# Two-layer hybrid decoder step on one core: fifth product kept in its own tile, and three reorderings in the in-product stage

## The chip, the cores and the metric

The kernel runs on one core of a Trainium2 chip. The metric is the device time of one execution in microseconds (us), as the median of several runs. One execution was also profiled; its rows are what the argument is made from.

## What is computed

Two layers. Layer 0 mixes tokens with two convolution mixers, layer 1 with dilated sliding-window attention; each layer ends in a ConvFFN, and a last RMSNorm follows. The change touches only the ConvFFN:

```python
def conv_ffn(h, st, w_in, wc, w_down):
    z = h @ w_in                                   # 1024 -> 2 * 2816
    g, st_new = causal_dwconv(z[..., :D_FF], st, wc)   # width 3, per channel
    return (jax.nn.silu(g) * z[..., D_FF:]) @ w_down, st_new
```

There are 1056 token columns (1024 of the prompt, 8 samples of 4 tokens), kept as three thirds of 352 columns. `h` is the normalised input of the layer; the kernel multiplies by the RMS factor (`rst`) after the product.

## The kernel before

**The in-product stage.** The 2816 channels of `z` are made in 22 rounds (`NJ`), j = 0 to 21, in each layer. One round makes 128 gate and 128 up channels for all tokens. It uses a recursive scheme with eleven block products in place of twelve. Each product is 12 TensorE matmuls of 352 columns (4 pieces of the contraction times 3 pieces of split precision), so a round has 132. In TensorE's order they are: P1, G3A, U3A, P5, P2, G3B, P6, P3, P7, U3B, P4 (the `STEP_...` constants; `step_full` counts them). P1, P6, P7 and P4 add up in one PSUM tile `za`, P5 and P3 in `ZB`, P2 in `ZC`, G3A and G3B in `ZG`, U3A and U3B in `zu`. `za` and `zu` alternate between two places from round to round.

**Operands.** Eight weight blocks are made ready for each round, one round ahead: A11, A21, A12, A22 straight from `w_raw`, and four sums S1, S2, S4, S3 that VectorE makes (`quad_sum`, S2 with two instructions). For each block ScalarE rounds the high part (`quad_hi`, L1283) and GpSimd takes the low part (`quad_lo`, L1710). P6 uses S2, P3 uses S4, P7 uses S3, U3B and P4 use A22.

**Intermediate results.** ScalarE copies three partial sums out of PSUM (`copy_part`, L1296): number 0 is `za` after P1, number 1 is `ZB` after P5, number 2 is `za` after P6. P6 waits for copy 0, P3 for copy 1, P7 for copy 2. VectorE then combines (`combine`): number 0 (L2069) after P2, 1 (L2076) after G3B, 2 (L2079) after P3, 3 (L2082, tile `u2`) after P7; P4 waits for combine 3. Combine 0 also has to precede copy 2, which overwrites `part`.

**Behind the products.** `scale_gate` (L2090) multiplies the gate by the factor, `taps` (L2101 to L2111) applies the width-3 convolution, ScalarE applies SiLU (`silu`, L1485), GpSimd multiplies by the factor (`silu_scale`, L1730), and VectorE multiplies by the up branch (`hidden`, L2131, three instructions, the last of which reads `u2`). `hidden(j-1)` falls in round j. The result `tmp` is stored by a DMA on SP's queue (`store_hid`), and reloaded for the down projection (`load_hid`, L609). The last round has a few instructions of the down projection mixed in: `hidden_lo(0, 0)` stands on VectorE ahead of combine 3 and needs the reload.

Every engine executes its instructions in the order in which they are written out by hand; semaphores join the engines. In the trace the tile `u2` appears as `u`, and `ZB` and `za` as `reg`; `ob` is the second place of `zu`. The line that the argument turns on is in `copy_part`, for copy 1:

```python
if which == 1:
    act.wait_ge(prod_ok, 3 * jj)      # all three instructions of hidden(j-1)
    dst, src = u2[:, :], ZB
```

Of the kernel before, what the change touches and what calls it, by code (L numbers as in the profile page):

```python
# [22 lines left out]
F32 = mybir.dt.float32  # L23
# [175 lines left out]
def build(nc, xT, wstream, par, ident_d, ones_d, stA, stB, stF, kva, kvb, wtab, sbias, cache_k, cache_v,  # L199
# [3 lines left out]
    with ExitStack() as ctx:  # L203
        def place(name, shape, dt, off):
            size = int(np.prod(shape[1:])) * 4
            return nc.alloc_sbuf_tensor_at(name, shape, dt, offset=off), off + (size + 31) // 32 * 32
# [34 lines left out]
        spare, off = place("spare", [P, T], F32, off)  # L241
        mean_s, off = place("mean_s", [P, NS], F32, off)
        cs, off = place("cs", [P, 16], F32, off)
        prod, off = place("prod", [P, NB, NQ // 2, KA], F32, off)
        AS, off = place("AS", [P, CA, NB, PAD + NQ], F32, off)
        tmp, off = place("tmp", [P, T], F32, off)
# [1 line left out]
        acc, off = place("acc", [P, T], F32, off)  # L248
        assert off <= nc.sbuf_usable_end
        gbuf = g3  # L250
        rst2, o2 = place("rst2", [P, T], F32, SX0)
        assert o2 <= SX0 + 4 * NJ * NB * (KF - 1 + NQ)
        sf_st, o2 = place("sf_st", [P, NJ, NB, KF - 1], F32, SPARE0)
# [986 lines left out]
        def _(act):  # L1240
# [44 lines left out]
            def copy_part(L, j, which):  # L1285


                jj = NJ * L + j
                act.wait_ge(step_full, step_at(L, j, (STEP_P1, STEP_P5, STEP_P6)[which]))
                if which == 1:  # L1290
                    act.wait_ge(prod_ok, 3 * jj)
                    dst, src = u2[:, :], ZB
                else:
                    act.wait_ge(comb_ok, 4 * jj + 1 if which else max(4 * jj - 1, 0))
                    dst, src = part[:, :], ZA[j % 2]
                nc.scalar.activation(dst, src, ACT.Copy).then_inc(part_ok, 1)  # L1296
# [181 lines left out]
            def ffn(L):  # L1478
                first_tiles(L)

                def silu(j):
                    jj = NJ * L + j
                    act.wait_ge(conv_ok, jj + 1)
                    act.wait_ge(prod_ok, 3 * jj)
                    nc.scalar.activation(sil[:, PAD:], acc[:, :], ACT.Silu).then_inc(silu_ok, 1)  # L1485

                def down_hi(d):


                    u = U_FFN[L] + 2 * NJ + d  # L1490
                    act.wait_ge(step_full, step_at(L, NJ - 1, (STEP_G3B, STEP_P3, STEP_P4)[d]))
                    split_hi(act, u)

                def hidden_hi(g):
                    act.wait_ge(hid_in[g % 2], 32 * ((6, 5)[g % 2] * L + g // 2 + 1))
                    for c in range(2):
                        nc.scalar.activation(hid[:, g % 2, c, 0, :], hraw[:, g % 2, c, 1, :], ACT.Copy).then_inc(hid_hi, 1)

                def last_copy():


                    act.wait_ge(step_full, step_at(L, NJ - 1, STEP_P4))
                    for x, z in enumerate((ZA, ZU)):
                        nc.scalar.activation(up_last[:, x, :], z[(NJ - 1) % 2], ACT.Copy).then_inc(last_up, 1)

                for j in range(NJ):
                    more = j < NJ - 1
                    if j > 0:
                        copy_part(L, j, 0)
                        quad_hi(L, j, Q_S3)  # L1510
                        quad_hi(L, j, Q_A22)
                        copy_part(L, j, 1)
                        if more:
                            quad_hi(L, j + 1, Q_A11)
                        else:
                            down_hi(0)
                        copy_part(L, j, 2)
                        if more:
                            quad_hi(L, j + 1, Q_A21)
                    if more:  # L1520
                        for q in (Q_S1, Q_A12, Q_S2, Q_S4):
                            quad_hi(L, j + 1, q)
                    else:
                        hidden_hi(0)
                        down_hi(1)
                        last_copy()
                        down_hi(2)
                    silu(j)
                hidden_hi(1)
                for g in range(NG - 1):  # L1530
                    for x in range(2):
                        hi_after(act, down_unit(L, g, x))
                    if g + 2 < NG:
                        hidden_hi(g + 2)
                s2 = 2 if L == 0 else 4
                for m in range(KD):
                    if L == 1 and m == KD - 1:
                        act.wait_ge(sum_ok, SQ0[4] + m - 1)
                        for t in range(NT):
                            act.wait_ge(h_third, t + 1)  # L1540
                            nc.scalar.activation(sqb[(SQ0[4] + m) % 2][:, t * TS:(t + 1) * TS],
                                                 h[:, m, t * TS:(t + 1) * TS], ACT.Square).then_inc(sq_third, 1)
                        return
                    h_ready(act, s2, m)
                    square(s2, m, h[:, m, :])
                    if L == 0:
                        gain_hi(2, 2, m)
                    if m % 4 == 3:
                        hi_after(act, down_unit(L, NG - 1, m // 4))
# [128 lines left out]
        def _(pool):  # L1678
# [34 lines left out]
            def ffn(L):  # L1713
# [14 lines left out]
                def silu_scale(j):  # L1728
                    pool.wait_ge(silu_ok, NJ * L + j + 1)
                    nc.gpsimd.tensor_tensor(sil[:, PAD:], sil[:, PAD:], rst[:, :], ALU.mult).then_inc(silr_ok, 1)  # L1730

                s = (1, 3)[L]
                for m in range(KD):
                    if m % 2 == 0 or L == 1:
                        lo_after(pool, U_OUT + 4 + m // 2 if L == 0 else U_WO + m)
                    add_square(s, m)
                for j in range(NJ):
                    if j > 0:
                        quad_lo(L, j, Q_S3)
                        quad_lo(L, j, Q_A22)  # L1740
                        silu_scale(j - 1)
                    if j < NJ - 1:
                        for q in (Q_A11, Q_A21, Q_S1, Q_A12):
                            quad_lo(L, j + 1, q)
                        if j > 0:
                            history(j)
                        for q in (Q_S2, Q_S4):
                            quad_lo(L, j + 1, q)
                        if j == 0:
                            history(j)  # L1750
                    else:
                        split_lo(pool, down_unit(L, 0, 0))
                        history(j)
                        silu_scale(j)
                        split_lo(pool, down_unit(L, 0, 1))
                        split_lo(pool, down_unit(L, 1, 0))
# [34 lines left out]
        def _(dve):  # L1791
# [219 lines left out]
            def ffn(L):  # L2011
# [48 lines left out]
                def combine(j, which):  # L2060


                    jj = J0 + j
                    dve.wait_ge(step_full, step_at(L, j, (STEP_P2, STEP_G3B, STEP_P3, STEP_P7)[which]))
                    if which == 0:
                        dve.wait_ge(part_ok, 3 * jj + 1)
                        dve.wait_ge(conv_ok, jj)
                        dve.wait_ge(hist_ok, 3 * jj)
                        ins = nc.vector.tensor_tensor(third(gbuf[:, PAD:], 0), ZC, part[:, :], ALU.add)  # L2069
                    elif which == 1:  # L2070
                        dve.wait_ge(hist_ok, 3 * jj)
                        g = third(gbuf[:, PAD:], 2)
                        if j == 0:
                            ins = nc.vector.tensor_copy(g, ZG)
                        else:
                            ins = nc.vector.tensor_tensor(g, ZG, third(rst, 2), ALU.mult)  # L2076
                    elif which == 2:
                        dve.wait_ge(part_ok, 3 * jj + 3)
                        ins = nc.vector.tensor_tensor(third(gbuf[:, PAD:], 1), ZB, part[:, :], ALU.add)  # L2079
                    else:  # L2080
                        dve.wait_ge(part_ok, 3 * jj + 2)
                        ins = nc.vector.tensor_tensor(u2[:, :], ZA[j % 2], u2[:, :], ALU.add)  # L2082
                    ins.then_inc(comb_ok, 1)

                def scale_gate(j):
# [113 lines left out]
                for j in range(NJ):  # L2199
# [11 lines left out]
                    if not more:  # L2211
                        hidden_lo(0, 0)
                    combine(j, 3)
                    if more:
                        quad_sum(j + 1, Q_S2)
                    else:
                        hidden_lo(0, 1)
                    if j == 0:
                        factor_parts((5, 9)[L])
                        quad_sum(1, Q_S4)  # L2220
                        scale_gate(0)
                    taps(j)
                    if more and j > 0:
                        quad_sum(j + 1, Q_S4)
                for g in range(NG - 1):
                    for x in range(2):
# [327 lines left out]
```

## Time and profile before

| what | value |
|---|---|
| median of 3 runs | 2655.68 us (2654.19 to 2655.82) |
| the profiled execution | 2654.6 us, span of the trace 2652.8 us |
| TensorE matmul busy | 2547.8 us, 96% of the span |
| VectorE, ScalarE, GpSimd busy | 1651.5 (62%), 798.5 (30%), 946.4 us (36%) |
| mean granted TensorE clock | 0.988 |
| chain that ended last | TensorE 64%, VectorE 16%, GpSimd 11%, issue 6% |

The span is the time between the first and the last instruction in the trace; the execution's own time is 1.8 us longer. The granted clock is a share of TensorE's full clock (1.0 is 2.4 GHz, 0.5 is 1.2 GHz). The in-product stage lies at about 376 to 881 us in layer 0, and 1868 to 2373 us in layer 1.

### The profile page before, as it was taken

What the parts mean: (1) busy time and instruction counts of PE and PEld (TensorE: products, weight loads), DVE (VectorE), ACT (ScalarE), POOL (GpSimd) and SP (SyncE); (2) the same over time, 40 slices, a digit from 0 to 9 for tenths busy, and PEclk for the clock granted to TensorE, in tenths of its full rate; (3) what the DMA queues carried; (4) which work ended last, traced back from release to release, by engine and by line L of the source; (5) the groups of instructions that cost most, each with busy time, mean ns of one, the idle gap of its engine ahead of it and who ended that gap; (6) DMA issues with size and microseconds to landing.
All of it is one profiled execution on the core that took longest, in us unless ns stands there. A gap on an engine that the chain in (4) does not pass through costs nothing.

```text
span 2652.8 us, 41667 instructions
## 1 busy us (share of the span) xinstructions
PE 2547.8 (96%) x17036; PEld 2379.0 (90%) x17036; DVE 1651.5 (62%) x2593; ACT 798.5 (30%) x1400; POOL 946.4 (36%) x635
## 2 busy tenths in 40 slices
PE   8999988999999999999999999989799999999997
PEld 8999987999999999987777777769799999999997
DVE  6999777666655655565565555564756556655555
ACT  5111343333333211233333333343433333331112
POOL 1000125666666322241000101123366666652222
PEclk9999998999999999999999999999999999999998
DMA  4111102444443544435344444432187888874321
GB/s 150 42 39 48 43 9 65 139 138 140 136 137 135 192 163 153 160 137 174 121 158 152 131 172 143 167 121 100 32 262 264 268 278 262 273 272 167 97 74 74
DMA packets 106557, 383.93 MB, mean 145 GB/s; under 512 B 23936, under 2 KB 41216, under 8 KB 103936
## 3 DMA queue, kind: packets, MB, share of 16 engines
q1 hardware_dynamic: 106368, 381.26, 43.3%
q8 instruction: 136, 2.23, 0.3%
q14 instruction: 53, 0.43, 0.1%
HBM read 339.15 MB, written 176.04 MB: 194 GB/s over the span
## 4 chain that ended last, share of the span: by engine, by line
PE 64%; DVE 16%; POOL 11%; issue 6%; ACT 2%; DMA 1%; DVEq 0%; SPq 0%; ACTq 0%; POOLq 0%
PE reg L824 19%; PE reg L771 11%; PE reg L1080 9%; PE reg L968 8%; POOL wq L1710 8%; DVE acc L2103 4%; POOL sil L1730 3%; PE reg L897 3%; PE reg L1060 3%; PE ob L1116 3%; DVE wqr L2044 2%; DVE tmp L2131 2%; PE reg L1033 1%; PE reg L1101 1%; PE ob L1101 1%
## 5 line engine op out<-in xcount | busy, mean ns | idle before, releaser
L968 PE MATMUL reg<-xo,wq 128*128 128x352 f32 x5280 | 877.0, 326 | 52.0 <-ACT u L1296 21.8
L968 PEld LDWEIGHTS reg<-xo,wq 128*128 128x128 f32 x5280 | 855.6, 190 | 67.1 <-ACT u L1296 33.7
L824 PE MATMUL reg<-hid,w_sp 128*128 128x352 f32 x3150 | 510.3, 324 | 0.5 <-DVE h L1830 0.5
L824 PEld LDWEIGHTS reg<-hid,w_sp 128*128 128x128 f32 x3150 | 509.9, 189 | 0.8 <-issue 0.8
L485 POOL TENSOR_TENSOR w_sp<-w_raw,w_sp 128x1024 fp32r<-128x1024 f32 x63 | 174.4, 2770 | 745.9 <-ACT w_sp L480 725.5
L1830 DVE TENSOR_TENSOR h<-reg,h 128x1056 f32<-128x1056 f32 x199 | 250.1, 1257 | 275.3 <-PE reg L824 225.6
L1710 POOL TENSOR_TENSOR wq<-wqr,wq 128x512 fp32r<-128x512 f32 x168 | 254.2, 1533 | 183.5 <-DVE wqr L2048 177.5
L771 PE MATMUL reg<-xs,w_sp 128*128 128x352 f32 x1872 | 308.6, 326 | 10.4 <-DVE xs L1819 9.7
L771 PEld LDWEIGHTS reg<-xs,w_sp 128*128 128x128 f32 x1872 | 304.3, 189 | 13.6 <-issue 13.1
L1710 POOL TENSOR_TENSOR wq<-w_raw,wq 128x512 fp32r<-128x512 f32 x168 | 242.1, 1450 | 148.6 <-ACT wq L1283 148.6
L1080 PE MATMUL reg<-xs,w_sp 128*128 128x352 f32 x1512 | 279.5, 332 | 0.4 <-DVE VT L2257 0.4
L1080 PEld LDWEIGHTS reg<-xs,w_sp 128*128 128x128 f32 x1512 | 240.5, 188 | 18.1 <-issue 18.0
L1283 ACT ACTIVATE wq<-wqr 128x512 fp32r<-128x512 f32 x176 | 110.7, 629 | 376.1 <-DVE wqr L2045 185.5
L480 ACT ACTIVATE w_sp<-w_raw 128x1024 fp32r<-128x1024 f32 x83 | 87.8, 1058 | 449.0 <-PE reg L824 291.0
L503 POOL TENSOR_TENSOR w_sp<-w_raw,w_sp 128x1024 fp32r<-128x1024 f32 x21 | 50.0, 2379 | 475.8 <-ACT w_sp L498 456.6
L2131 DVE TENSOR_TENSOR tmp<-reg,sil 128x352 f32<-128x352 f32 x64 | 31.5, 521 | 287.8 <-POOL sil L1730 287.8
L1583 ACT ACTIVATE pT<-ob 128x512 f32<-128x512 f32 (+1 forms) x96 | 47.1, 491 | 329.0 <-PE ob L1101 329.0
L2103 DVE SCALAR_TENSOR_TENSOR acc<-g,pt,acc 128x1024 f32<-128x1024 f32 x88 | 115.1, 1308 | 3.1
L1283 ACT ACTIVATE wq<-w_raw 128x512 fp32r<-128x512 f32 x176 | 109.8, 626 | 17.3 <-PE reg L968 17.2
L2298 DVE COPY pT<-reg 128x512 f32<-128x512 f32 (+1 forms) x96 | 53.4, 557 | 97.8 <-PE reg L1101 97.3
L2275 DVE CUSTOM_DVE_ANT_0 neg_s<-reg,wt 128x512 f32<-128x512 f32 (+1 forms) x192 | 107.3, 559 | 6.9 <-DVE eps L2263 0.3
L1576 ACT ACTIVATE neg_s<-neg_s,nmx 128x896 f32<-128x896 f32 (+7 forms) x128 | 98.1, 768 | 35.9 <-DVE nmx L2280 33.2
(248 smaller groups left out, 2972.8 us busy)
## 6 DMA issues: line engine op xcount, KB each, us to landing
w_raw<-in_wstream SPq DMA_DIRECT2D x192, 512.0 KB, 3.6
out_sv<-in_cache_v SPq DMA_DIRECT2D x16, 4088.0 KB, 16.0
out_sk<-in_cache_k SPq DMA_DIRECT2D x16, 4088.0 KB, 16.2
kvr<-in_kva SPq DMA_DIRECT2D x16, 2048.0 KB, 9.0
kvr<-in_kvb SPq DMA_DIRECT2D x16, 1536.0 KB, 7.0
hid_spill<-tmp SPq DMA_DIRECT2D x44, 528.0 KB, 3.0
hraw<-hid_spill SPq DMA_DIRECT2D x44, 528.0 KB, 4.5
wt<-in_wtab SPq DMA_DIRECT2D x16, 512.0 KB, 5.3
```

The source lines that it names most:

```text
L480: nc.scalar.activation(w_sp[:, u % 3, 0, :], w_raw[:, u % 3, :], ACT.Copy).then_inc(w_hi, 1)
L485: nc.gpsimd.tensor_tensor(w_sp[:, u % 3, 1, :], w_raw[:, u % 3, :], w_sp[:, u % 3, 0, :].bitcast(F32), ALU.subtract).then_inc(w_lo, 1)
L771: mm = nc.tensor.matmul(out[:, t, :], w[:, wh, k * P:(k + 1) * P], xs[:, xh, k, t * TS:(t + 1) * TS], start=(n == 0 and wh + xh == 0), sto ...
L824: mm = nc.tensor.matmul(out[:, t, :], w[:, wh, kk * 512 + m * P:kk * 512 + (m + 1) * P], hid[:, par_g, kk, xh, t * TS:(t + 1) * TS], start ...
L968: mm = nc.tensor.matmul(out, w[:, wh, k * P:(k + 1) * P], xo[:, o, xh, k, :], start=(first and k == 0 and wh + xh == 0), stop=(k == 3 and ...
L1080: mm = nc.tensor.matmul(dense[:, t, :], w[:, wh, k * P:(k + 1) * P], xs[:, xh, k, t * TS:(t + 1) * TS], start=(k == 0 and wh + xh == 0), s ...
L1283: nc.scalar.activation(wq[:, ring(L, j, q), 0, :], quad_src(L, j, q), ACT.Copy).then_inc(wq_hi, 1)
L1576: nc.scalar.activation(neg_s[:, hh, 0:w], neg_s[:, hh, 0:w], ACT.Exp, bias=nmx[:, m, hh:hh + 1], scale=-1.0, accum_out=lsum[:, 0, hh:hh + ...
L1710: nc.gpsimd.tensor_tensor(wq[:, r, 1, :], quad_src(L, j, q), wq[:, r, 0, :].bitcast(F32), ALU.subtract).then_inc(wq_lo, 1)
L1830: nc.vector.tensor_tensor(tok(h[:, m, :]), region(r), tok(h[:, m, :]), ALU.add).then_inc(free, 1)
L2103: chain(nc.vector.scalar_tensor_tensor(out=y, in0=g, scalar=w[k], in1=y, op0=ALU.mult, op1=ALU.add))
L2275: nc.vector.tensor_tensor_reduce(out=neg_s[:, hh, lo:lo + w], in0=S[hh][:, 0:w], in1=wt[:, hh, t0:t0 + w], scale=-1.0, scalar=3.0e38, op0= ...
```

## The change

1. **Fifth product.** Copy 1 (P5) goes to a tile of its own, `p5`, laid over the storage of `prod`, which only layer 0's long convolution uses. It no longer waits for `hidden(j-1)`, but for the previous round's combine 3, which reads `p5`. Combine 3 now adds `p5` to `za` and writes `u2`.
2. **SiLU on ScalarE.** In rounds 2 to 21 `silu(j-1)` follows copy 0 of round j; before, it stood ahead of it. `silu(0)` follows copy 1 of round 1.
3. **Factor on GpSimd.** In rounds 2 to 21 `silu_scale(j-1)` stands ahead of the low parts of S3 and A22 instead of behind them. In round 1 nothing is moved.
4. **Taps on VectorE.** `taps(j)` stands ahead of both instructions of `quad_sum(j+1, S2)` rather than behind them. In round 0 `quad_sum(1, S4)` moves ahead of `factor_parts` (the two reciprocals).

```diff
+        p5, o2 = place("p5", [P, TS], F32, PROD0)
...
                 if which == 1:
-                    act.wait_ge(prod_ok, 3 * jj)
-                    dst, src = u2[:, :], ZB
+                    act.wait_ge(comb_ok, 4 * jj)
+                    dst, src = p5[:, :], ZB
...
                     if j > 0:
                         copy_part(L, j, 0)
+                        if j > 1:
+                            silu(j - 1)
                         quad_hi(L, j, Q_S3)
                         quad_hi(L, j, Q_A22)
                         copy_part(L, j, 1)
+                        if j == 1:
+                            silu(0)
...
-                    silu(j)
+                        silu(j)
...
                 for j in range(NJ):
+                    if j > 1:
+                        silu_scale(j - 1)
                     if j > 0:
                         quad_lo(L, j, Q_S3)
                         quad_lo(L, j, Q_A22)
-                        silu_scale(j - 1)
+                    if j == 1:
+                        silu_scale(0)
...
                         dve.wait_ge(part_ok, 3 * jj + 2)
-                        ins = nc.vector.tensor_tensor(u2[:, :], ZA[j % 2], u2[:, :], ALU.add)
+                        dve.wait_ge(prod_ok, 3 * jj)
+                        ins = nc.vector.tensor_tensor(u2[:, :], ZA[j % 2], p5[:, :], ALU.add)
...
                     combine(j, 3)
-                    if more:
-                        quad_sum(j + 1, Q_S2)
-                    else:
+                    if not more:
                         hidden_lo(0, 1)
                     if j == 0:
+                        quad_sum(1, Q_S2)
+                        quad_sum(1, Q_S4)
                         factor_parts((5, 9)[L])
-                        quad_sum(1, Q_S4)
                         scale_gate(0)
                     taps(j)
                     if more and j > 0:
+                        quad_sum(j + 1, Q_S2)
                         quad_sum(j + 1, Q_S4)
```

ScalarE, the turn from round 1 to round 2 of layer 0, before: L1485 is `silu(1)`, the first `part` copy 0 of round 2, `u_75` copy 1; the two instructions between them are the high parts of S3 and A22.

```order
L1283 ACTIVATE wq<-wqr 128x512 x2
L1485 ACTIVATE sil<-acc 128x1056
L1296 ACTIVATE part<-reg 128x352
L1283 ACTIVATE wq<-wqr 128x512
L1283 ACTIVATE wq<-w_raw 128x512
L1296 ACTIVATE u_75<-reg 128x352
```

The same place after the change (L1299 is the copy, L1488 SiLU, L1286 the high part, `p_73` the new tile):

```order
L1286 ACTIVATE wq<-wqr 128x512 x2
L1299 ACTIVATE part<-reg 128x352
L1488 ACTIVATE sil<-acc 128x1056
L1286 ACTIVATE wq<-wqr 128x512
L1286 ACTIVATE wq<-w_raw 128x512
L1299 ACTIVATE p_73<-reg 128x352
```

SiLU has changed places with copy 0; the copy of the fifth product stands where it stood. In round 1 of a layer, after the change, ScalarE has this (copy 0, the two high parts, copy 1, a load of the activation table, `silu(0)`, the high part of round 2's A11, copy 2):

```order
L1299 ACTIVATE part<-reg 128x352
L1286 ACTIVATE wq<-wqr 128x512
L1286 ACTIVATE wq<-w_raw 128x512
L1299 ACTIVATE p_73<-reg 128x352
L1488 ACT_TABLE_LOAD
L1488 ACTIVATE sil<-acc 128x1056
L1286 ACTIVATE wq<-w_raw 128x512
L1299 ACTIVATE part<-reg 128x352
```

Before, the table load and `silu(0)` stood ahead of all of these. GpSimd, a later turn of rounds, before: the low parts of S2, S4 and S3, that of A22, then the factor (L1730).

```order
L1710 TENSOR_TENSOR wq<-wqr,wq 128x512 x3
L1710 TENSOR_TENSOR wq<-w_raw,wq 128x512
L1730 TENSOR_TENSOR sil<-sil,rst 128x1056
L1710 TENSOR_TENSOR wq<-w_raw,wq 128x512 x2
```

After the change (L1717 the low part, L1737 the factor):

```order
L1717 TENSOR_TENSOR wq<-wqr,wq 128x512 x2
L1737 TENSOR_TENSOR sil<-sil,rst 128x1056
L1717 TENSOR_TENSOR wq<-wqr,wq 128x512
L1717 TENSOR_TENSOR wq<-w_raw,wq 128x512 x3
```

The factor now has two low parts fewer ahead of it in this turn, and S3 and A22 have it ahead of them.

## Rows read from the trace of the kernel before

**Rows 1.** Windows, all rounds between the stage's start and end, both layers

```profile
core 0: us, PE busy (x) PEld busy (x) DVE busy (x) ACT busy (x) POOL busy (x), PEclk, DMA share, GB/s
440.00:860.00 420.00, 412.75 (x2556) 407.58 (x2555) 254.94 (x370) 128.08 (x231) 287.47 (x229) 1.00 0.43 134
1932.00:2352.00 420.00, 412.82 (x2559) 407.65 (x2558) 254.39 (x370) 128.81 (x232) 288.68 (x231) 1.00 0.81 267
```

**Rows 2.** Chain that ended last: start us, us, what (TensorE without a wait)

```profile
440.11 27.07 PE reg L968 x168
```

**Rows 3.** Timeline of one round, layer 0: start us, us, engine, instruction, [idle before]

```profile
553.56 0.69 DVE L2048 TENSOR_TENSOR wqr<-w_raw,wqr 128x512 f32<-128x512 f32 x1
...
554.40 4.12 POOL L1710 TENSOR_TENSOR wq<-wqr,wq 128x512 fp32r<-128x512 f32 x3 [4.08 <-DVE wqr L2048]
...
558.48 1.29 POOL L1710 TENSOR_TENSOR wq<-w_raw,wq 128x512 fp32r<-128x512 f32 x1
559.74 2.05 POOL L1730 TENSOR_TENSOR sil<-sil,rst 128x1056 f32<-128x1056 f32 x1
561.82 0.96 DVE L2131 TENSOR_TENSOR tmp<-reg,sil 128x352 f32<-128x352 f32 x2 [6.96 <-POOL sil L1730]
...
563.30 0.46 ACT L1296 ACTIVATE u<-reg 128x352 f32<-128x352 f32 x1 [6.02 <-DVE tmp L2131]
...
563.82 4.14 PE L968 MATMUL reg<-xo,wq 128*128 128x352 f32 x24 [0.36 <-ACT u L1296]
...
568.00 0.52 DVE L2082 TENSOR_TENSOR u<-reg,u 128x352 f32<-128x352 f32 x1 [0.18 <-PE reg L968]
568.45 1.07 DVE L2044 TENSOR_TENSOR wqr<-w_raw 128x512 f32<-128x512 f32 x1
...
569.55 1.67 DVE L2045 TENSOR_TENSOR wqr<-wqr,w_raw 128x512 f32<-128x512 f32 x1
...
571.14 0.74 DVE L2101 TENSOR_SCALAR acc<-g,pt 128x1024 f32<-128x1024 f32 x1
...
571.92 2.61 DVE L2103 SCALAR_TENSOR_TENSOR acc<-g,pt,acc 128x1024 f32<-128x1024 f32 x2
```

**Rows 4.** Timeline, rounds 0 and 1 of layer 0

```profile
407.87 6.54 DVE L1812 RECIPROCAL rst<-rst 128x1024 f32<-128x1024 f32 x1
...
416.21 1.28 ACT L1485 ACT_TABLE_LOAD   x1
...
418.42 3.59 DVE L2103 SCALAR_TENSOR_TENSOR acc<-g,pt,acc 128x1024 f32<-128x1024 f32 x2
...
424.79 3.89 PE L968 MATMUL reg<-xo,wq 128*128 128x352 f32 x12 [6.35 <-ACT part L1296]
...
431.89 6.29 PE L968 MATMUL reg<-xo,wq 128*128 128x352 f32 x24 [3.22 <-ACT u L1296]
...
438.02 2.09 PE L968 MATMUL ob<-xo,wq 128*128 128x352 f32 x12
```

**Rows 5.** Timeline, the same place in layer 1

```profile
1917.26 3.89 PE L968 MATMUL reg<-xo,wq 128*128 128x352 f32 x12 [5.34 <-ACT part L1296]
...
1929.86 2.07 PE L968 MATMUL ob<-xo,wq 128*128 128x352 f32 x12
```

**Rows 6.** Windows, rounds 1 (from P6 on), both layers; columns as in rows 1

```profile
424.79:431.89 7.10, 3.88 (x12) 3.43 (x12) 1.99 (x5) 1.49 (x4) 4.53 (x3) 0.50 0.48 148
...
1917.26:1924.37 7.11, 3.89 (x12) 3.44 (x12) 2.00 (x5) 1.50 (x4) 4.53 (x3) 0.70 0.48 150
```

**Rows 7.** Timeline, the last round of layer 0

```profile
868.43 1.20 SPq L609 DMA_DIRECT2D hraw<-hid_spill  x2
...
868.59 4.14 PE L968 MATMUL reg<-xo,wq 128*128 128x352 f32 x24 [0.49 <-ACT u L1296]
...
874.60 2.06 ACT L1497 ACTIVATE hid<-hraw 128x1056 fp32r<-128x1056 f32 x2 [4.76 <-DMA hraw<-hid_spill]
...
877.46 3.51 PE L968 MATMUL reg<-xo,wq 128*128 128x352 f32 x12 [2.81 <-DVE u L2082]
```

**Rows 8.** Timeline, the last round of layer 1

```profile
2369.21 3.89 PE L968 MATMUL reg<-xo,wq 128*128 128x352 f32 x12 [3.33 <-DVE u L2082]
```

More of the change, by code:

```diff
@@ L243, in build @@
         cs, off = place("cs", [P, 16], F32, off)
+        PROD0 = off
         prod, off = place("prod", [P, NB, NQ // 2, KA], F32, off)
@@ L250, in build @@
         gbuf = g3
+        p5, o2 = place("p5", [P, TS], F32, PROD0)
+        assert o2 <= PROD0 + 4 * NB * (NQ // 2) * KA
         rst2, o2 = place("rst2", [P, T], F32, SX0)
```

## The prediction

> **What bounds the stage now.** I read the windows first, to see how much TensorE has left to gain. Between the stage's ragged start and end, 420 us hold 2556 matmuls [rows 1], 21.69 us for a round of 132. Where nothing holds TensorE, 168 matmuls take 27.07 us [rows 2], 161.1 ns each, so a round at its pace is 21.27 us. The granted clock is 1.00 throughout. The missing 0.4 to 0.5 us a round is a wait, and it is all that the change can win in a steady round.
>
> Then one round's timeline, for what closes the loop [rows 3]. The last sum S4 is made at 553.56. GpSimd takes four low parts (S2, S4, S3, A22) from 554.40 to 559.77, and the factor until 561.80. Only then can `hidden` run, whose third instruction frees `u2` at 563.2; ScalarE copies the fifth product at 563.30, and P3, the first half of the 24 matmuls at 563.82, starts 0.36 us late. P7 ends at 567.98, combine 3 runs, and S2, taps and S4 follow on VectorE until the next low parts start one round later. So a loop VectorE, GpSimd, VectorE, ScalarE, TensorE sets the period, a little above TensorE's own. VectorE and GpSimd are busy for 255 and 287 of 420 us [rows 1]: it is their order that binds.
>
> Last, the ragged ends. In round 1 TensorE idles 6.35 us before P6, because ScalarE holds copy 0 behind `silu(0)`, then 3.22 us before P3 [rows 4]; the layer-1 idle before P6 is 5.34 us [rows 5]. The clock falls with it: 0.50 in 424.79:431.89 [rows 6], P6's 12 matmuls take 3.89 us instead of 1.93. In the last round P4 waits 2.81 us (3.33 in layer 1) and then takes 3.51 (3.89) us [rows 7, 8].
>
> **Steady rounds.** I count time t from P7's end. In the new loop combine 3 ends at t+0.47; taps follow. Their stretch cost 0.74 + 2.61 + about 0.8 us for the samples [rows 3]. In their new place three low parts and the state copies of GpSimd run beside them, where S2's instructions now take 1.07 and 1.67 us against 0.69 for the like S4 [rows 3]. The nearest row for taps beside GpSimd is the pair in round 0, 3.59 us against 2.61 [rows 4, 3]. I add 1.3 us to taps and take 1.3 off S2, which moves out of that place: S4 ends at t+8.0, as before (553.56+0.69 against P7's end one period before). GpSimd: S2 and S4 low (half of the 5.37 us that the four take) until t+10.8, the factor until t+12.8. SiLU is ready: after S4's high part (0.6) and copy 0 (0.45), 1.07 us, t+10.3. `hidden` and combine 0: 1.4 + 0.43, until t+14.7. Nothing on TensorE waits for `hidden` now but through combine 0, copy 2 and P7. Copy 2 needs P6, which ends at t+17.4 (nine products after P7: U3B, P4, then seven of the next round), and P7 starts at t+19.3. Even with the 0.5 of the copy there are 4.1 us between the chain and P7. Copy 1 (P5 ends at t+11.6) has until P3, t+17.4; S3's and A22's low parts, now behind the factor, end at t+15.5, needed at 19.3 and 21.3. The weight reload behind A22's low part leaves 1.9 us later; its block is wanted in the round after next, and hides. So steady rounds are TensorE's, 21.27 us. From P4 of round 1 (438.02 + 1.93 = 439.95) to P3 of round 21 (868.59) [rows 4, 7] lie 428.64 us and 12 + 19·132 + 84 = 2604 matmuls, 419.6 us at the pace: **9.0 us** a layer, 18.0 in both.
>
> **Start of the stage.** S4 of round 1 no longer stands behind the reciprocals (6.54 us [rows 4]), and copy 0 not behind `silu(0)`, so P6 starts without a wait at 418.44 and ends at 420.4. P3 needs copy 1, behind the high parts of S3 and A22, and S3's sum stands on VectorE behind taps(0): reciprocals until 415.5, `scale_gate` until 416.8, taps (beside less of GpSimd than now, 4.5 us) until 421.3, S3 422.0, two high parts and the copy until 423.6. P3 starts 8.2 us sooner than now. But P7 is behind a longer chain: table load 1.28 us, SiLU 1.07, the factor 2.05, `hidden` 1.4, combine 0, copy 2: 430.45. The idle time of 3.2 us before P3 becomes 4.9 before P7. No row has exactly this idle; 5.34 and 6.35 us were each followed by 12 matmuls at the lower clock (3.89 us) [rows 4, 5], so I take P7 at 3.87. P4 of round 1 then starts at 430.45 + 3.87 + 1.93 = 436.3 in place of 439.95: **3.7 us**. In layer 1 the chain is the same 1492.4 us later: 1928.7 against 1929.86 + 1.93 = 1931.8: **3.1 us**. Bounds: P7 at full clock, 1.9 more a layer; U3B slow as well, 1.9 less.
>
> The table load is now on this path; its row is 1.28 us [rows 4], which the sum uses. The Trainium skill (ScalarE: Activation LUTs, What ACT_TABLE_LOAD costs) adds a drain of about 1.38 us to the 1.28 of the load. By that page, as an estimate, the start would gain 1.4 us less a layer and the kernel take 2.8 us longer than forecast.
>
> **End of the stage.** The chain is `hidden(20)`, store, reload (868.43 to 874.60 [rows 7]), high and low part, combine 3, P4. `hidden(20)` ends two low parts sooner, some 2.7 us, and the reload is behind it in SP's queue and behind nothing else. Combine 3 comes at about 874.2 in place of 876.9, U3B ends near 873.9: P4 waits 0.4 us, in layer 1, by the same count, 0.95. With so short a wait I take P4 at full clock, 1.93 us. Gains: 2.4 + 1.6 = **4.0** and 2.4 + 1.9 = **4.3 us**. If the clock falls all the same, 3.5 less in all. In the down projection behind it VectorE's chain (taps, SiLU, factor, `hidden(21)`) moves up with combine 3; I take nothing for it, at most 1 us lost.
>
> **Sum.** 18.0 + 3.7 + 3.1 + 4.0 + 4.3 = 33.1 us off the profiled execution's 2654.6: 2621.5. The median of the runs lies 1.1 above that execution: **2622.5 us**. The rest (`p5` for `u2` as target and source) changes no duration: the same sizes and memories.
>
> **Rivals.** (a) *The loop closes again, shorter.* Taps or low parts run slower side by side than I have them, and half of the steady gain stays lost: 2631.5. It needs 4.1 us more in the chain than counted before it bites, and 4.3 to halve the gain; the rows show 1.0 us for the pair. 0.08. (b) *The change doesn't do what it says in steady rounds*: the 0.4 us is TensorE's own gap at this place, or another wait (S4's low part) ends there too. Then only the ends gain, 15.1 us: 2640.5. Against it, P3's idle ends with the copy, and the other operands have been ready for over 4 us. 0.05. (c) *Slower.* Taps are put beside GpSimd's low parts, and each of the three long ones waits for a whole GpSimd instruction of up to 1.9 us, S2 as much as now: 5.7 − 1.3 + 1.3 + 1.7 for GpSimd's own low parts is 7.4 us, 3.3 over the slack of 4.1, a period of 24.6 us, 2.8 more than now in 39 rounds: +109, less 15 at the ends, 2750. It decides from 4.6 us on. The pair in round 0 lost only 1.0 us beside the same work [rows 4]. 0.04. The Trainium skill (SBUF — State Buffer, SBUF: two separate sides) has it that a VectorE instruction with two SBUF inputs and a GpSimd one exclude each other for the whole instruction; by that rule (c) is what would happen, and the trace agrees in the sign (1.67 against 0.69 us for one of S2), not in the size here. (d) Losses and gains cancel within 0.2%, which is what a measurement of this kernel can tell: needs 28 us of the 33 lost, 0.02. My forecast has 0.81.
>
> **Range.** Downwards: P7 at full clock in both layers (3.9) and no wait at the end (1.4) give 2617; with half a per mille of the measurement, 2615. Upwards: U3B slow too (3.9), P4's clock lost (3.5), 1 us in the down projection, and (a) half: 2634. Faster than by 0.2%: 0.94; within it 0.02; slower 0.04.
>
> **What would show it.** Steady windows: 2556 matmuls in 412 us, no wait of TensorE on a ScalarE copy. `hidden`'s wait for the factor falls from 6.96 to some 4 us. Round 1: one idle of about 3 us before P3, one of about 5 before P7, released by copy 2, and a stretch at clock 0.5 behind it. P4 of round 21 with a wait under 1 us and 1.93 us long. I am wrong if a steady round keeps a wait before P7 or P3, if taps take much over 5.5 us, or if the clock falls elsewhere.

## The result, and the profile after

The changed kernel takes 2626.94 us (median of 4 runs, 2623.84 to 2632.76), the kernel before 2655.68: a ratio of 0.9896, interval 0.9875 to 0.9916, 28.7 us less. The forecast was 2622.5, range 2615 to 2634. The profiled execution is the slowest of the four, 2632.76 us (span 2631.0), 21.8 less than the profiled one of before.

The windows of the steady rounds, changed kernel, columns as in [rows 1]:

```profile
440.00:850.00 410.00, 410.00 (x2547) 410.00 (x2546) 256.28 (x369) 130.25 (x232) 294.67 (x229) 1.00 0.45 137
1932.00:2342.00 410.00, 410.00 (x2547) 410.00 (x2546) 252.76 (x364) 129.31 (x229) 294.37 (x230) 1.00 0.78 270
```

TensorE is busy in all of the 410 us, where it had been in 412.8 of 420. The chain that ended last shows the same; it now stays on TensorE from one product to the next:

```profile
438.84 27.07 PE reg L971 x168
...
481.37 27.07 PE reg L971 x168
```

Two rounds are 42.53 us, 21.27 each, as the pace of [rows 2] gives. One round's timeline, against [rows 3]:

```profile
564.94 0.51 DVE L2093 TENSOR_TENSOR u<-reg,p 128x352 f32<-128x352 f32 x1
565.37 1.35 DVE L2112 TENSOR_SCALAR acc<-g,pt 128x1024 f32<-128x1024 f32 x1
...
566.76 2.60 DVE L2114 SCALAR_TENSOR_TENSOR acc<-g,pt,acc 128x1024 f32<-128x1024 f32 x2
...
571.67 0.69 DVE L2058 TENSOR_TENSOR wqr<-w_raw,wqr 128x512 f32<-128x512 f32 x1
...
572.51 2.86 POOL L1717 TENSOR_TENSOR wq<-wqr,wq 128x512 fp32r<-128x512 f32 x2 [4.42 <-DVE wqr L2058]
...
575.34 2.05 POOL L1737 TENSOR_TENSOR sil<-sil,rst 128x1056 f32<-128x1056 f32 x1
...
576.14 0.47 ACT L1299 ACTIVATE p<-reg 128x352 f32<-128x352 f32 x1 [0.74 <-PE reg L971]
...
577.42 0.53 DVE L2142 TENSOR_TENSOR tmp<-reg,sil 128x352 f32<-128x352 f32 x1 [4.45 <-POOL sil L1737]
...
578.94 0.51 DVE L2079 TENSOR_TENSOR g<-reg,part 128x352 f32<-128x352 f32 x1
...
581.94 0.47 ACT L1299 ACTIVATE part<-reg 128x352 f32<-128x352 f32 x1 [4.82 <-PE reg L971]
```

Read it from combine 3 at 564.94, which starts 0.4 us after P7's end. S4 ends at 572.4, 7.4 us on; two low parts and the factor end at 577.4; combine 0 ends at 579.45, 14.95 us after P7's end (14.7 counted). The copy of the fifth product, at 576.14, and copy 2, at 581.94, each wait for a product of TensorE, no longer for VectorE.

The start of the stage in layer 0, against [rows 4], and the same places in layer 1, against [rows 5]:

```profile
408.91 1.57 DVE L2058 TENSOR_TENSOR wqr<-w_raw,wqr 128x512 f32<-128x512 f32 x1
...
413.39 7.79 PE L971 MATMUL reg<-xo,wq 128*128 128x352 f32 x48
425.06 1.28 ACT L1488 ACT_TABLE_LOAD   x1
425.09 3.89 PE L971 MATMUL reg<-xo,wq 128*128 128x352 f32 x12 [3.91 <-ACT p L1299]
426.35 1.08 ACT L1488 ACTIVATE sil<-acc 128x1056 f32<-128x1056 f32 x1
...
432.22 3.89 PE L971 MATMUL reg<-xo,wq 128*128 128x352 f32 x12 [3.24 <-ACT part L1299]
435.91 2.93 PE L971 MATMUL ob<-xo,wq 128*128 128x352 f32 x12
...
1907.25 2.20 PE L971 MATMUL reg<-xo,wq 128*128 128x352 f32 x12 [2.86 <-ACT p L1299]
...
1914.38 3.89 PE L971 MATMUL reg<-xo,wq 128*128 128x352 f32 x12 [4.93 <-ACT part L1299]
```

P5 to P6 run through (the 48 matmuls), then P3 and P7 wait, and P7 is slow in both layers, P3 in one. The windows over P3, P7 and U3B of layer 0 and over P3 and P7 of layer 1 show which clock they had (the third figure from the end):

```profile
424.70:429.00 4.30, 3.89 (x12) 3.43 (x12) 0.00 (x0) 3.23 (x4) 3.54 (x3) 0.50 0.57 168
...
432.00:436.00 4.00, 3.78 (x13) 3.78 (x14) 2.76 (x4) 1.82 (x4) 3.24 (x3) 0.50 0.33 135
436.00:438.80 2.80, 2.80 (x14) 2.80 (x13) 2.62 (x3) 0.00 (x0) 2.80 (x4) 0.69 0.00 0
...
1907.20:1909.40 2.20, 2.15 (x12) 1.91 (x12) 0.00 (x0) 2.18 (x2) 1.72 (x2) 1.00 0.51 209
1914.30:1918.20 3.90, 3.82 (x13) 3.82 (x14) 2.62 (x3) 1.69 (x4) 3.28 (x3) 0.50 1.10 392
```

The end of the stage in layer 0, against [rows 7]: P4's wait, then the down projection with a wait of its own.

```profile
865.23 2.17 PE L971 MATMUL reg<-xo,wq 128*128 128x352 f32 x12 [1.07 <-DVE u L2093]
...
867.24 11.76 PE L827 MATMUL reg<-hid,w_sp 128*128 128x352 f32 x72
...
873.72 5.06 POOL L488 TENSOR_TENSOR w_sp<-w_raw,w_sp 128x1024 fp32r<-128x1024 f32 x2
874.40 4.76 DVE L2142 TENSOR_TENSOR tmp<-xraw,sil 128x352 f32<-128x352 f32 x2
...
880.91 19.37 PE L827 MATMUL reg<-hid,w_sp 128*128 128x352 f32 x109 [1.91 <-DVE h L1840]
```

### The profile page after: what moved, and what is told of

Same layout as the page of the kernel before. It is cut to its first block, busy times and chain, and to the rows that moved or that the text cites. A ratio compares the mean times of both kernels' runs of the same rounds, so it can differ in the third digit from the quotient of the medians.

```text
span 2631.0 us, 41669 instructions
## 1 busy us (share of the span) xinstructions
PE 2545.5 (97%) x17036; PEld 2387.4 (91%) x17036; DVE 1657.9 (63%) x2593; ACT 802.9 (31%) x1400; POOL 956.5 (36%) x635
## 4 chain that ended last, share of the span: by engine, by line
PE 88%; DVE 7%; issue 2%; ACT 1%; DMA 1%; POOL 1%; DVEq 0%; SPq 0%; ACTq 0%; POOLq 0%
PE reg L971 29%; PE reg L827 19%; PE reg L774 11%; PE reg L1083 9%; PE ob L971 3%; PE reg L900 3%; PE reg L1063 3%; PE ob L1119 3%; PE reg L1036 1%; PE reg L1104 1%; PE ob L1104 1%; PE reg L1172 1%; PE reg L1159 1%; DVE neg_s L2286 1%; PE reg L794 1%
## 5 line engine op out<-in xcount | busy, mean ns | idle before, releaser
L1717 POOL TENSOR_TENSOR wq<-wqr,wq 128x512 fp32r<-128x512 f32 x168 | 232.3, 1393 | 180.0 <-DVE wqr L2058 173.1
L1717 POOL TENSOR_TENSOR wq<-w_raw,wq 128x512 fp32r<-128x512 f32 x168 | 253.1, 1516 | 111.2 <-ACT wq L1286 111.1
L1286 ACT ACTIVATE wq<-wqr 128x512 fp32r<-128x512 f32 x176 | 110.5, 628 | 383.5 <-DVE wqr L2055 338.9
L2142 DVE TENSOR_TENSOR tmp<-reg,sil 128x352 f32<-128x352 f32 x64 | 31.5, 521 | 188.1 <-POOL sil L1737 188.1
L1286 ACT ACTIVATE wq<-w_raw 128x512 fp32r<-128x512 f32 x176 | 109.4, 624 | 17.7 <-PE reg L971 17.3
```

The lines of the kernel that those rows point to most:

```text
L1286: nc.scalar.activation(wq[:, ring(L, j, q), 0, :], quad_src(L, j, q), ACT.Copy).then_inc(wq_hi, 1)
L1717: nc.gpsimd.tensor_tensor(wq[:, r, 1, :], quad_src(L, j, q), wq[:, r, 0, :].bitcast(F32), ALU.subtract).then_inc(wq_lo, 1)
```

## The experiments

Twelve kernels, each but `b4_slack` in five rounds beside the kernel before. "Undone" is meant from the changed kernel.

| label | what | median us | ratio to before, 95% |
|---|---|---|---|
| a1_full_again | the changed kernel | 2627.1 | 0.9895 (0.9880 to 0.9910) |
| a2_tile_only | only the own tile | 2628.0 | 0.9901 (0.9888 to 0.9915) |
| a3_factor_only | only the factor's place | 2630.3 | 0.9906 (0.9892 to 0.9919) |
| a4_taps_only | only VectorE's order | 2660.1 | 1.0020 (1.0011 to 1.0029) |
| b1_no_tile | own tile undone | 2625.4 | 0.9888 (0.9874 to 0.9901) |
| b2_taps_back | taps undone | 2625.9 | 0.9893 (0.9873 to 0.9912) |
| c1_s4_back | S4 of round 1 undone | 2626.5 | 0.9888 (0.9875 to 0.9902) |
| c2_silu_back | SiLU undone in rounds 2 to 21 | 2624.0 | 0.9885 (0.9871 to 0.9898) |
| b3_start_and_end | rounds 1 and 21 reordered | 2616.7 | 0.9854 (0.9841 to 0.9868) |
| c3_start | round 1 reordered | 2617.3 | 0.9856 (0.9838 to 0.9874) |
| c4_start_end_split | both, and hidden(21) spread | 2608.9 | 0.9826 (0.9807 to 0.9844) |
| b4_slack | three factor instructions more | 2862.0 | 1.0779 (1.0759 to 1.0799) |

**a1_full_again.** No edit.

> The changed kernel once more, for the spread of its runs and a second profile. Theory A (what remains of the gain varies with when TensorE's clock falls and rises around the short idle times at the stage's ends): steady rounds again 21.27 us with no wait, the medians near 2627 us, single runs between 2622 and 2633, and the second profile differs from the first in stretches at the lower clock, not in a wait. Rival B (a transfer or a wait that is late in some runs): the second profile shows one wait of several us that the first doesn't have, or the other way round.

The four runs go from 2623.7 to 2629.1, and no wait of the stage or of the down projection differs by more than 1.6 us from the first profile's (layer 1's wait in the down projection, 1.9 us instead of 0.3). One wait is new, 0.7 us before P4 of round 11 in layer 0, behind a weight block that came late. But neither theory names the larger difference, TensorE's own pace in the steady rounds. The first profile has 168 matmuls in 27.07 us throughout; the second, in layer 0:

```profile
440.36 26.69 PE reg L971 x168
```

That is 158.9 ns a matmul against 161.1, at a granted clock of 1.00 in both. The layer's 2604 matmuls take 414.7 us instead of 419.5, with the wait of 0.7 in them: 4.8 of the 6.3 us between the two profiles. Other profiles have 26.88, and b1's changes within a layer with no wait between. The first stage of the kernel, 504 matmuls in 81.53 us, is the same in every profile. What sets the pace stays open. It can hide or feign a gain of a few us in a median of four runs, so each run below is read by its trace as well, in stretches from one product to another.

**One part alone.** a2 has the lines of the change that make and use `p5` and nothing more, a3 only the factor's place:

```diff
                 for j in range(NJ):
+                    if j > 1:
+                        silu_scale(j - 1)
                     if j > 0:
                         quad_lo(L, j, Q_S3)
                         quad_lo(L, j, Q_A22)
-                        silu_scale(j - 1)
+                    if j == 1:
+                        silu_scale(0)
```

and a4 only VectorE's order (the last part of the change).

> Only the fifth product's own tile; SiLU, factor, taps and sums stand as before the change. Theory A (the chain counted from P7's end reaches copy 2 at 17.9 us, 1.4 us ahead of P7 even with four low parts in it): steady rounds at TensorE's pace, all of the 18 us; start 1 to 3 us a layer, since P3 no longer waits for the u2 tile but P6 still for SiLU; P4 of the last round waits still over 3 us. About 2633 us (2630 to 2638). Rival B (the order of the factor is what matters, the tile alone only shifts the wait to copy 2): steady rounds stay above 21.5 us, over 2642 us.

> Only the factor moved ahead of the low parts of S3 and A22 on GpSimd (rounds 2 to 21); no own tile, SiLU, taps and sums as before the change. Theory A (the chain to copy 1 gets 2.6 us shorter, ends at 14.8 us from P7's end, P3 needs it at 17.4): steady rounds at TensorE's pace, all of the 18 us; start as before the change; end as in the whole change. About 2631 us (2627 to 2637). Rival B (only the tile breaks the loop): a copy of the fifth product still ends a wait of P3, less than 6 us gained.

> Only VectorE's order changed (taps ahead of S2, and S4 of round 1 ahead of the reciprocals). Theory A (the loop holds taps, S2 and S4 in whatever order, and SiLU stands behind S4's high part): steady rounds as before, 21.7 us; the start 1 us a layer faster; about 2653 us (2650 to 2657). Rival B (earlier taps free SiLU and with it the factor): at least 8 us faster, 2647 or less.

Theory A held in the first two: TensorE has no wait from 440 to 850 us in either. The tile alone brings 26.7 us and the factor's place alone 24.4, against 27.6 for the whole change beside the same runs of before; the intervals overlap. a2 came out 5 us better than its point and 2 below its range. Part is the faster pace in layer 1 (26.88 us), part the start: from P4 of round 0 to P4 of round 1 it takes 31.6 and 30.5 us in the two layers, the whole change 33.0 and 31.5, the kernel before 35.1 and 33.4. In a2 nearly all the idle time falls ahead of P6 (6.2 us in layer 0). P7 waits 1.4 us and runs at a granted clock of 1.00:

```profile
432.14 2.18 PE L971 MATMUL reg<-xo,wq 128*128 128x352 f32 x12 [1.41 <-ACT part L1299]
```

So at the start the whole change loses to the tile alone, 1.4 and 1.0 us in the two layers (1.2 and 0.4 by a1's profile): it starts P7 1.2 us sooner, but as a slow product. It wins at the end, where a2's P4 still waits 3.2 and 2.9 us.

In a4 both theories were too kind: it is slower. All waits of its TensorE for ScalarE from 404 to 895 us, and the kernel before's:

```profile
PE reg L971 <- ACT u L1299: 15.6, 19, 3.2
PE reg L971 <- ACT part L1299: 3.9, 1, 3.9
```

```profile
PE reg L968 <- ACT u L1296: 10.9, 19, 3.2
PE reg L968 <- ACT part L1296: 6.4, 1, 6.4
```

The start gains 2.4 us in layer 0, by the shorter wait before P6; in layer 1 that wait stays (5.2 against 5.3 us) and the start loses 1.0. The waits for the copy of `u2` grow by 0.25 us a round and the steady rounds by 0.2 us (432.3 and 432.0 us from P4 of round 1 to P3 of round 21, against 428.6 and 428.0). a4's timeline shows why:

```profile
740.98 1.15 DVE L2105 TENSOR_SCALAR acc<-g,pt 128x1024 f32<-128x1024 f32 x1
741.54 1.74 POOL L1714 TENSOR_TENSOR wq<-w_raw,wq 128x512 fp32r<-128x512 f32 x1
742.16 3.51 DVE L2107 SCALAR_TENSOR_TENSOR acc<-g,pt,acc 128x1024 f32<-128x1024 f32 x2
...
745.84 0.24 DVE L2113 TENSOR_SCALAR acc<-sx,pt 128x32 f32<-128x32 f32 x1 [0.16 <-POOL sf_st L1730]
```

Taps begin while GpSimd works on low parts and states; two of them take 3.51 us instead of 2.61, and they end 5.7 us after their start instead of 4.2. S2 gains most of that back, not all: S4 ends 8.3 us after combine 3's start, 8.1 in the kernel before.

**One part undone.** b1 takes the tile away:

```diff
-                    act.wait_ge(comb_ok, 4 * jj)
-                    dst, src = p5[:, :], ZB
+                    act.wait_ge(prod_ok, 3 * jj)
+                    dst, src = u2[:, :], ZB
```

with `silu(0)` behind copy 0 of round 1; b2 puts `quad_sum(j + 1, Q_S2)` ahead of `taps(j)` again; c1 puts `factor_parts` ahead of `quad_sum(1, Q_S4)` again; c2 puts `silu(j - 1)` ahead of `copy_part(L, j, 0)` again for j > 1.

> The whole change without the fifth product's own tile: copy 1 goes to u2 again and waits for hidden(j-1); SiLU, factor and VectorE's order as changed (silu(0) behind copy 0 of round 1, where the wait needs it). Theory A (the tile and the factor's place are two ways to the same gain): steady rounds at TensorE's pace; P3 of round 1 is 6 us later than in the whole change, P7 4 us later, P4 1 to 2; about 2630 us (2626 to 2635). Rival B (the tile carries the gain of the whole): over 2640 us.

> The whole change with S2 ahead of taps again in all rounds (S4 of round 1 stays ahead of the reciprocals). Theory A (the order of taps and S2 changes the chain by some tenths of a us, and there is slack of over 3): as the whole change, 2627 us (2624 to 2630). Rival B (taps ahead is what makes room for the factor): a wait of P3 or P7 in steady rounds, over 2635 us.

> The whole change with S4 of round 1 behind the reciprocals again (the only edit undone). Theory A: P6 of round 1 needs S2's low part, which waits for S4's sum; that sum then comes 6.9 us later, its low part about when P6 is due, so P6 waits 0 to 2 us and is covered by P7's longer wait; VectorE reaches taps(0) at the same time. 2627 us (2624 to 2631). Rival B (the S4 move carries the start): P4 of round 1 over 2 us a layer later, 2631 or more.

> The whole change with SiLU ahead of copy 0 again in rounds 2 to 21 (the only edit undone). Theory A: SiLU is ready 0.4 us sooner, copy 0 comes 1.1 us later and isn't due for 5 us; steady rounds at TensorE's pace, 2627 us (2624 to 2630), in the spread of the whole change. Rival B (copy 0 behind SiLU delays P6): a wait of TensorE for the copy in steady rounds, over 2632 us.

All four medians lie between 2624.0 and 2626.5, within the whole change's spread (b1's 0.6 us below its range), and in steady rounds TensorE never waits for a copy; c1 and c2 have one short wait each, 0.3 and 0.7 us, at the place of a1's. So for the steady rounds each single part can be missing, the tile too. In b1's layer 0, P3 of round 1 waits 10.0 us instead of 3.9 and P7 then none: the two short idles have become one long one, and P4 of round 1 comes no later (32.8 us after P4 of round 0, 33.0 in the whole change); in layer 1 it comes 0.8 us later. In c1, P6 doesn't wait at all, as Theory A's lower bound had it, but P3 of layer 1 waits 5.1 us instead of 2.9, and P4 of round 1 comes 0.3 us later in layer 0 and 1.8 in layer 1. c1's median doesn't show these 2 us, because its steady rounds ran at a faster pace (413.8 us in layer 1 against 419.5). So the S4 move is worth about 2 us by the traces, less than its first place in my count of the start's gain.

**b4_slack.** How much later may the chain get? GpSimd multiplies by the factor four times instead of once, so the hidden values differ from the reference's.

```diff
+                    for n in range(3):
+                        nc.gpsimd.tensor_tensor(sil[:, PAD:], sil[:, PAD:], rst[:, :], ALU.mult).then_inc(again, 1)
+                        pool.wait_ge(again, 3 * (NJ * L + j) + n + 1)
                     nc.gpsimd.tensor_tensor(sil[:, PAD:], sil[:, PAD:], rst[:, :], ALU.mult).then_inc(silr_ok, 1)
```

> The whole change with three more factor instructions of GpSimd in each round's chain (the values of the up branch are multiplied by the factor four times, so they differ), 6.2 to 6.5 us more between SiLU and hidden. Theory A (the chain has 3.7 us of slack before P7): the period rises by 2.5 to 2.8 us to about 23.9, P7 waits for copy 2, some 105 us more in all, 2730 us (2715 to 2745). Rival B (the slack is under 2 us): over 2795 us. Rival C (GpSimd is free enough that hidden is not in the way): under 2680 us.

```profile
PE reg L971 <- ACT part L1299: 48.3, 15, 4.9
...
617.73 12.52 PE L971 MATMUL reg<-xo,wq 128*128 128x352 f32 x60 [3.34 <-ACT part L1299]
...
617.70:630.00 12.30, 12.27 (x60) 12.28 (x61) 10.25 (x13) 2.39 (x5) 9.07 (x9) 0.76 0.36 89
```

By its time the run says rival B, by its trace Theory A's place and nearly its size. P7 waits for copy 2, in 15 rounds 3.2 us each on the mean. The chain is longer by more than the 6.4 us of the three instructions: GpSimd's low parts now fall beside the taps, whose pair takes mostly 3.5 to 4.4 us instead of 2.6, and from P7's end to combine 0's end it is 21.7 to 23.4 us from round 3 on, 14.95 in the changed kernel. In round 10 of layer 0 it is 6.9 us more, and P7 waits 3.3: the slack was 3.6 us. The changed kernel's own trace gives the same: with the 0.6 us that b4 shows from combine 0's end to P7's start, its P7 could start 3.6 us sooner. 3.7 had been expected and 4.1 stood in the prediction. What no theory had priced is the clock: 60 matmuls behind a wait take 12.5 us instead of 9.7, and the clock over them is 0.76. The round is 26.2 us, 4.9 more: 3.2 of idle and the rest slow matmuls.

**b3, c3, c4: what is left at the ends.** Round 1 on ScalarE and VectorE, in all three:

```diff
                         copy_part(L, j, 0)
                         if j > 1:
                             silu(j - 1)
+                        else:
+                            copy_part(L, j, 1)
                         quad_hi(L, j, Q_S3)
                         quad_hi(L, j, Q_A22)
-                        copy_part(L, j, 1)
-                        if j == 1:
+                        if j > 1:
+                            copy_part(L, j, 1)
+                        else:
                             silu(0)
...
                         quad_sum(j, Q_S3)
-                        hidden(j - 1)
+                        if j > 1:
+                            hidden(j - 1)
                         combine(j, 0)
...
                     if j > 0:
                         scale_gate(j)
+                    if j == 1:
+                        hidden(0)
```

b3 and c4 also have `combine(21, 3)` ahead of `hidden_lo(0, 0)`. c4 spreads `hidden(21)`, one of its three instructions behind each of the additions 2, 3 and 4:

```diff
-                            if g == 0 and x == 0 and m == 1:
-                                hidden(NJ - 1)
+                            if g == 0 and x == 0 and m >= 1:
+                                hidden(NJ - 1, (m - 1,))
```

> The whole change, and in round 1 copy 1 ahead of the high parts of S3 and A22, the combines 0 to 2 and the gate's scaling ahead of hidden(0); in round 21 combine 3 ahead of hidden_lo(0, 0). Theory A (P3 of round 1 waits for taps(0) only by VectorE's and ScalarE's order, P7 for hidden(0) likewise): P3 starts with no wait, P7 waits 2 to 3 us for S3's low part, P4 of round 1 starts 4 to 7 us sooner than in the whole change in each layer; the end gains 0 to 2 us. About 2616 us (2611 to 2621). Rival B (the clock takes it back: the idle time moves to P4 and is followed by slow matmuls all the same): under 5 us in all, 2622 or more.

> The whole change with the new order of round 1 alone (copy 1 ahead of the high parts, combines 0 to 2 ahead of hidden(0)), not combine 3 ahead of hidden_lo in round 21. Theory A (all of the 10 us that the two edits brought come from round 1; P4's wait at the end only moves to the down projection's wait for VectorE): 2617 us (2614 to 2620). Rival B (both share): 2619 or more, with P4 of round 21 slow behind its wait.

> The edits of round 1 and round 21 together, and hidden(21), three instructions that stand in a row between the second and the third addition of the down projection, spread out: one behind each of the additions 2, 3 and 4. Theory A (TensorE's 2.6 us wait for the third addition is due to these three, 3.2 to 4.8 us together beside GpSimd): the wait falls under 0.5 us, 2 us a layer and up to 1.6 of clock behind it: 2612 us (2608 to 2616). Rival B (the additions themselves wait for TensorE, so the wait only comes later): 2616 or more.

Start and down projection of layer 0 in b3, then in c4:

```profile
428.79 3.89 PE L971 MATMUL reg<-xo,wq 128*128 128x352 f32 x12 [3.90 <-ACT part L1299]
...
432.48 2.64 PE L971 MATMUL ob<-xo,wq 128*128 128x352 f32 x12
...
PE reg L827 <- DVE h L1843: 2.6, 1, 2.6
```

```profile
PE reg L971 <- ACT part L1299: 4.8, 1, 4.8
PE reg L827 <- DVE h L1843: 0.6, 1, 0.6
```

P3 has no wait any more; one wait of 3.9 us, for copy 2, is left of two with 7.2, and behind it P7 is slow and U3B in part. Copy 2 is now behind `silu(0)` on ScalarE, not behind `hidden(0)`. P4 of round 1 comes 5.6 us sooner in layer 0 but only 2.4 in layer 1, where 4 to 7 had been expected. b3 and c3 come out alike (2616.7, 2617.3): P4's wait of round 21, taken away, returns as a longer wait for VectorE's additions, 2.6 us against 1.9. Spreading `hidden(21)` cuts that to 0.6 in layer 0 and to nothing in layer 1, and c4 is 7.8 us below b3, 18 below the changed kernel. The down projections alone are 3.2 and 4.1 us shorter in c4's trace than in b3's; 4.6 of these 7.3 are the waits (2.0 and 2.6), the rest is matmuls that took longer in b3.

## Why the prediction was right, and where it was off

**Steady rounds: right in mechanism and size.** From P4 of round 1 to P3 of round 21 layer 0 went from 428.6 us to 419.5, 9.1 less (9.0 forecast), layer 1 from 428.0 to 419.5, 8.5 less. Rivals (a), (b) and (c) did not come: no wait in these rounds. The measured slack is 3.6 us, where the text has 4.1. But a shorter chain was not what mattered: a2 and a3 show that four low parts in the chain with the tile, or the copy of `u2` with the factor moved, fit as well. Two edits that each break the loop add nothing to each other in its rounds. The prediction gave the gain to all the edits together and didn't say so.

**Taps: the sign of a term was wrong in the loop.** I took the exchange with S2 as even, 1.3 us against 1.3. In a4, where the loop binds, it costs 0.2 us a round. In the whole change GpSimd is done with its low parts sooner, and the pair takes 2.6 us in all but 3 of 38 rounds: S4 ends 7.4 us after combine 3's start, against 8.1 before, and a3, with S2 still ahead, reaches 7.3. Rival (c)'s size is refuted: beside GpSimd the three long taps of a4 take 4.7 us instead of 3.4, not 5.7 us more. The Trainium skill's rule (SBUF — State Buffer, SBUF: two separate sides) is mutual exclusion for whole instructions. The traces agree in that both slow down when they meet: the taps' pair takes 3.51 us instead of 2.61, and GpSimd's low part 1.74 instead of 1.28.

**Start of the stage: right shape, mis-sized in both layers.** P3 and P7 wait as forecast. From P4 of round 0 to P4 of round 1, layer 0 gained 2.1 us (3.7 forecast) and layer 1 1.8 (3.1). P7 started 26.6 us after the start of round 0's P4; 25.6 had been counted, as S4's sum beside GpSimd took 1.57 us where I had 0.69; layer 1 has the same 1.0 us. And U3B was slow too, 2.93 us in layer 0 and 2.59 in layer 1, a bound that I had named. The table load took its 1.28 us and SiLU began 0.01 us later. The Trainium skill (ScalarE: Activation LUTs, What ACT_TABLE_LOAD costs) adds a drain of about 1.38 us to a load. It doesn't show here.

**End of the stage: too hopeful.** P4 waited 1.07 and 1.78 us (0.4 and 0.95 forecast) and took 2.17 and 2.72. The stage's end gained 3.2 and 2.8 us, where 4.0 and 4.3 had been expected. In layer 0 `hidden(20)` ends 2.1 us sooner against P3 of round 21, where 2.7 had been counted; it now runs beside GpSimd's low parts, with its third instruction 0.73 us long.

**Down projection: the step that failed.** I let VectorE's chain move up with combine 3 and took nothing for it, at most 1 us. In the profiled execution it gave back 2.9 us in layer 0 and 0.5 in layer 1. Against TensorE the chain had moved back: P4 behind combine 3 is no longer slow, so the down projection starts 2.6 us after combine 3 and not 3.9. SiLU and the factor come 1.3 us later against it, and so do the two long low parts of the down weights behind them on GpSimd. `hidden(21)` starts 7.2 us after the down projection's first matmul in both kernels, but the two low parts end 4.4 us after its start and not 3.0. The kernel before:

```profile
880.81 11.76 PE L824 MATMUL reg<-hid,w_sp 128*128 128x352 f32 x72
...
885.95 5.03 POOL L485 TENSOR_TENSOR w_sp<-w_raw,w_sp 128x1024 fp32r<-128x1024 f32 x2
...
887.97 3.40 DVE L2131 TENSOR_TENSOR tmp<-xraw,sil 128x352 f32<-128x352 f32 x2
```

Now two of its instructions take 4.76 us, the third addition is late, TensorE waits 1.91 us instead of 0.55, and the next matmuls are slow (1512 in 245.93 us instead of 244.37; a2 has the same wait with 244.37 behind it). In layer 1 P4 and the first down matmuls were slow, the two instructions took 3.16 us, and the wait was 0.3 us. c4 tested the step from `hidden(21)` to the wait: with it spread, 0.6 us are left in layer 0 and nothing in layer 1. That the low parts' place makes it long is read from the traces alone.

**The sum.** 27.5 us by the stage's rows in place of 33.1. Of these 3.4 went in the two down projections and 2.3 in stretches that the change doesn't touch. That gives the 21.8 of the profiled pair. The medians' 28.7 lies nearer to the forecast because runs of the changed kernel differ by up to 9 us, and the profiled one is the slowest. Where a1 could be compared with it, the larger part of the difference was the pace, which the prediction had fixed at 161.1 ns. So that the median came within 4.4 us of the forecast is in part luck: the start, the end and the down projection together fell 8.6 us short, and a faster pace, as in a1's profile, made up for a part. The range's upper end is also added wrongly: its terms give 2635.4, not 2634.

## What to carry to other kernels

When several edits shorten one chain, ask which alone brings it under TensorE's own time: here either of two was enough, and the new place of the taps, worth nothing with them, made the kernel slower by itself. Once the steady part is bound by TensorE, the gain is in the first and last rounds: write them out in their own order, since the order that is right for a steady round can hold up an operand there that is due first. An idle of 3 us cost up to 6 here, as the clock behind it fell. And where runs of one kernel differ by more than an edit is worth, compare the traces from one product to another, not only the medians.

## What the runs showed of the hardware

- Unbroken runs of the stage's matmuls at a granted clock of 1.00 took 158.9, 160.0 or 161.1 ns each, by run and stretch; the 504 of the kernel's first stage took 81.53 us in every profile.
- Waits of 2.9 to 5 us before 12 matmuls were mostly, not always, followed by clock 0.50: 3.89 us after 3.91, 3.24 and 4.93, but 2.20 after 2.86, and in a2 2.17 after 3.20.
- One of VectorE's two-input instructions and one of GpSimd's side by side each took 1.3 to 2.3 times as long as alone (S4's sum 1.57 us against 0.69, the taps' pair 3.51 against 2.61, GpSimd's low part 1.74 against 1.28).
